# A two-block transformer layer in fp32 on one core: matmuls on high and low parts replaced by plain fp32 matmuls

## The reference

```
# block one
h = rms_norm(x, norm_mix_pre); q, k, v, u, gates = split(h @ w_in)            # 1024 -> 4096
y_a = chunk_band_attention(q, k, v, rel_bias) @ w_attn_out                    # 8 heads of 64
y_b = multiscale_pool(u, w_pool_group, pool_scale) @ w_pool_out
g_a, g_b = split(sigmoid(gates + b_gate))
x = x + rms_norm((g_a * y_a + g_b * y_b) @ w_o, norm_mix_post)
x = x + rms_norm(conv_gated_ffn(rms_norm(x, ..), w_up, conv_w, conv_b, w_down), ..)   # 1024 -> 2*2816 -> 1024
# block two
proj = rms_norm(x, g_mix) @ w_in_2                                            # 1024 -> 3072
h = x + concat(diff_attention(..), neighbourhood_attention(..)) @ w_out
h = h + hier_moe(rms_norm(h, g_ffn), w_rg, w_re, w1, w3, w2)                  # 32 experts, two a token
h = h + rms_norm(p @ w_ple, g_ple) * sigmoid(rms_norm(h, g_plg) @ w_plg)
```

## Time and profile before

| | us |
|---|---|
| median of 3 runs | 1834.44 (1833.17 to 1841.0) |
| the profiled execution | 1832.7 |
| its span, first to last instruction | 1830.9 |
| PE busy | 1599.6 (87%) |
| PE weight loads | 1128.8 (62%) |
| DVE busy | 737.1 (40%) |
| ACT busy | 534.2 (29%) |
| POOL busy | 210.3 (11%) |

### The profile page before, as it was taken

One profiled execution on the slowest core, in us unless ns is written; L12 is line 12 of the kernel. 1 busy time (PEld: TensorE's weight loads), 2 busy tenths in 40 slices (PEclk: granted clock), 3 DMA queues, 4 the chain that ended last, 5 costly groups with the idle time before them and its releaser, 6 DMA issues. The chain is left out here.

```text
span 1830.9 us, 19904 instructions
## 1 busy us (share of the span) xinstructions
PE 1599.6 (87%) x7826; PEld 1128.8 (62%) x7826; DVE 737.1 (40%) x1310; ACT 534.2 (29%) x1012; POOL 210.3 (11%) x204
## 2 busy tenths in 40 slices
PE   5999999879999999787987669698889889888859
PEld 5865688768888888565865558444345345333449
DVE  5225332364444444664439762411113113112363
ACT  4224322344333234332326671211011011010242
POOL 2032010022121111133120100200000000000010
PEclk9988999989999999888999899699999999999979
DMA  7210123113222223021210112468998999999711
GB/s 262 107 36 23 70 94 113 71 63 110 92 92 93 92 92 111 37 95 69 93 38 20 70 37 91 184 253 325 396 358 332 394 347 360 392 368 388 308 38 47
DMA packets 101469, 300.26 MB, mean 164 GB/s; under 512 B 4976, under 2 KB 7152, under 8 KB 90880
## 3 DMA queue, kind: packets, MB, share of 16 engines
q1 hardware_dynamic: 99968, 294.14, 43.1%
q0 software_dynamic: 1408, 4.83, 0.8%
HBM read 296.86 MB, written 2.10 MB: 163 GB/s over the span
## 5 line engine op out<-in xcount | busy, mean ns | idle before, releaser
L514 DVE TENSOR_TENSOR w_lo<-M,w_hi 128x2048 fp32r<-128x2048 f32 x73 | 167.6, 2308 | 215.1 <-ACT w_hi L509 215.1
L2037 PE MATMUL bank<-M 128*64 128x512 f32 x1024 | 229.3, 598 | 26.8 <-DMA M<-in_w 26.3
L699 PE MATMUL bank<-HTH,w_hi 128*128 128x512 f32 x576 | 225.0, 391 | 0.0
L699 PE MATMUL bank<-HTL,w_hi 128*128 128x512 f32 x576 | 224.6, 390 | 0.0
L699 PE MATMUL bank<-HTH,w_lo 128*128 128x512 f32 x576 | 224.5, 390 | 0.0
L509 ACT ACTIVATE w_hi<-M 128x2048 fp32r<-128x2048 f32 x73 | 138.5, 1910 | 192.2 <-PE bank L699 78.4
L2037 PEld LDWEIGHTS bank<-M 128*64 128x64 f32 x1024 | 75.8, 137 | 169.0 <-issue 167.6
L726 PE MATMUL bank<-w_hi,HTH 128*128 128x512 f32 x320 | 129.7, 405 | 20.4 <-DVE M L1400 9.8
L2052 PE MATMUL bank<-M 128*64 128x512 f32 x512 | 116.8, 603 | 25.5 <-DMA M<-in_w 25.0
L726 PE MATMUL bank<-w_lo,HTH 128*128 128x512 f32 x320 | 127.4, 398 | 0.0
L726 PE MATMUL bank<-w_hi,HTL 128*128 128x512 f32 x320 | 127.3, 398 | 0.0
(11 more groups left out here) (270 smaller groups left out, 2746.7 us busy)
## 6 DMA issues: line engine op xcount, KB each, us to landing
M<-in_w SPq DMA_DIRECT2D x192, 1024.0 KB, 11.7
M<-in_wd SPq DMA_DIRECT2D x78, 1024.0 KB, 4.8
M<-in_nb SPq DMA_DIRECT2D x4, 1536.0 KB, 6.3
X<-in_x SPq DMA_DIRECT2D x4, 512.0 KB, 7.6
M<-in_tb POOLq DMA_DIRECT2D x8, 256.0 KB, 4.4
out<-M SPq DMA_DIRECT2D x16, 128.0 KB, 1.9
rowb<-in_rows POOLq DMA_DIRECT2D x3, 512.0 KB, 3.9
M<-in_pT POOLq DMA_DIRECT2D x1, 512.0 KB, 5.2
```

What stands on the lines that cost most here:

```text
L514: e.tensor_tensor(lo[:, :], slots[slot_of[n]], hi[:, :], ALU.subtract).then_inc(split_lo_done, 1)
L699: m = e.matmul(out[:, :], w[:, k0 + k, n0:n0 + 128], v[k], start=(k == 0 and i == 0), stop=(k == len(hi) - 1 and i == 2))
L2037: m = e.matmul(b[64 * s:64 * s + 64, :], Xe[:, 4 * kh + k, o + C * s:o + C * s + C], unit_w(key, 4)[:, k, :], start=(kh == 0 and k == 0), ...
```

## The change

Every product of high and low parts becomes one plain fp32 matmul on the data itself. With it go the copies and subtractions of weights (`split_act`, `split_dve`), those of activations, and the second matmul of gather and scatter. The room they took holds longer rings: `NS` goes from 4 to 6, `NS_MOE` from 7 to 10, `NS_ONCE` from 5 to 2. A dense slot is now free when its matmuls have read it (`unit_read`) instead of when its low part is written. In the feed-forward part POOL writes its product straight into `A`. In the experts the second half of an output is read out of PSUM by DVE and the first by ACT; before, ACT read both for the high part and DVE both for the low part. Norms have one buffer a tile and end at the gain.

```
-NS = 4
+NS = 6
-NS_MOE = 7
-NS_ONCE = 5
+NS_MOE = 10
+NS_ONCE = 2
...
-        def gemm3_T(e, key, n0, out, fills, hi, lo, k0=0):
-            wh, wl = parts(key, KD)
-            for k in range(len(hi)):
-                for i, (w, v) in enumerate(((wh, hi), (wh, lo), (wl, hi))):
-                    m = e.matmul(out[:, :], w[:, k0 + k, n0:n0 + 128], v[k], start=(k == 0 and i == 0),
-                                 stop=(k == len(hi) - 1 and i == 2))
+        def gemm_T(e, w, n0, out, fills, src, k0=0):
+            for k, v in enumerate(src):
+                m = e.matmul(out[:, :], w[:, k0 + k, n0:n0 + 128], v, start=(k == 0), stop=(k == len(src) - 1))
             m.then_inc(fills, 1)
...
             for k in range(4):
-                for i, (src, w) in enumerate(((HTH, wh), (HTH, wl), (HTL, wh))):
-                    m = e.matmul(out[:, :], src[:, 4 * j + k, t * 128:(t + 1) * 128], w[:, k, :],
-                                 start=(j == k == i == 0), stop=(j == 1 and k == 3 and i == 2))
+                m = e.matmul(out[:, :], src[:, 4 * j + k, t * 128:(t + 1) * 128], w[:, k, :], start=(j == k == 0),
+                             stop=(j == 1 and k == 3))
...
         def load_dense(e, n):
             if n >= NS:
-                e.wait_ge(split_lo_done, n - NS + 1)
+                unit_read(e, keys[n - NS])
...
-            if s == 7 and R != 3:
-                e.wait_ge(n_hi, 2 * (NORM_N[R] + t + 1))
-                e.tensor_tensor(HTL[ht_place(t, 1)], norm_y(R, t, 1), HTH[ht_place(t, 1)], ALU.subtract).then_inc(n_lo_v, 1)
...
-            for n in range(8):
-                e.wait_ge(mixed, n + 1)
-                filled(e, ("g", 3, 1, 1))
-                e.activation(HTH[:, n, :], MT[:, n, :], ACT.Copy).then_inc(mt_hi, 1)
...
-            for n in range(8):
-                e.wait_ge(mt_hi, n + 1)
-                e.tensor_tensor(HTL[:, n, :], MT[:, n, :], HTH[:, n, :], ALU.subtract).then_inc(mt_lo, 1)
...
                             for t in range(TT):
-                                for q, v in enumerate((XSH, XSL)):
-                                    m = e.matmul(b[:, kk * 256:(kk + 1) * 256], v[:, t, k * 128:(k + 1) * 128], S[:, t, :],
-                                                 start=(t == 0 and q == 0), stop=(t == 3 and q == 1))
+                                m = e.matmul(b[:, kk * 256:(kk + 1) * 256], XS[:, t, k * 128:(k + 1) * 128], S[:, t, :],
+                                             start=(t == 0), stop=(t == 3))
...
                             for p in SCAT[i]:
-                                for q, Y in enumerate((YH, YL)):
-                                    m = e.matmul(b[:, :], ST[p % 6][:, t * 128:(t + 1) * 128], Y[p % 3][:, h * 512:(h + 1) * 512],
-                                                 start=(p == SCAT[i][0] and q == 0), stop=(p == SCAT[i][-1] and q == 1))
+                                m = e.matmul(b[:, :], ST[p % 6][:, t * 128:(t + 1) * 128], Y[p % 3][:, h * 512:(h + 1) * 512],
+                                             start=(p == SCAT[i][0]), stop=(p == SCAT[i][-1]))
```

More of the change, by code:

```diff
@@ L198, in area @@
             return mem(A0 + o, *shape)
+        HT, XS, S = mem(HT0, KD, NTOK), area(0, TT, D), area(8192, TT, 4 * C)
+        ST = [area(10240 + 512 * i, NTOK) for i in range(6)]
+        Y = [area(13312 + 1024 * i, D) for i in range(3)]
+        OS = area(20704, TT, C)
         o_st = [0]
@@ L567, in norm_act @@
                 e.activation(sq, ms, ACT.Sqrt).then_inc(n_sqrt, 1)
-            if s == 4 and R == 3:
-                e.wait_ge(n_scaled, 4 * R + t + 1)
-                filled(e, ("o2", 3, 1))
-                e.activation(XSH[:, t, :], norm_xs(R, t), ACT.Copy).then_inc(n_keep_hi, 1)
-            if s == 6 and R != 3:
-                if R == 1:
-                    filled(e, ("wo", 3, 1))
-                if R == 2:
-                    filled(e, ("dn", 4, 3, 1))
-                for h in range(2):
-                    taken(e, ("n", R, t, h))
-                    e.activation(HTH[ht_place(t, h)], norm_y(R, t, h), ACT.Copy).then_inc(n_hi, 1)
         def norm_dve(e, R, t, s):
@@ L1078, in wo_pe @@
                     m.then_inc(w_used, 1)
+            ws = [unit_in(e, ("wo", 2 + j), 4) for j in range(2)]
             for t in range(TT):
@@ L1745, in out2_pe @@
                     m.then_inc(w_used, 1)
+            ws = [unit_in(e, ("out2", 2 + j), 4) for j in range(2)]
             for t in range(TT):
@@ L2080, in moe_act @@
                         sc_done(e, i - 3)
-                    for h in range(2):
-                        b, _ = filled(e, ("y2", i, h))
-                        e.activation(YH[i % 3][:, h * 512:(h + 1) * 512], b[:, :], ACT.Copy, scale=WC[i]).then_inc(m_yh, 1)
+                    evac_act(e, Y[i % 3][:, 0:512], ("y2", i, 0), WC[i])
                 if what == "ple":
@@ L2400, in round_pe @@
         for k in range(KD):
-            for i, (t, x) in enumerate([(t, x) for t in range(TT) for x in XS]):
-                m = e.matmul(bank[0][:, k * C:(k + 1) * C], x[:, t, k * 128:(k + 1) * 128], S[:, t, :], start=(i == 0),
-                             stop=(i == 7))
+            for t in range(TT):
+                m = e.matmul(bank[0][:, k * C:(k + 1) * C], XS[:, t, k * 128:(k + 1) * 128], S[:, t, :], start=(t == 0),
+                             stop=(t == 3))
         m.then_inc(o_gath, 1)
```

493 lines of the change are left out of this document (135 added, 358 removed).

## The result

The changed kernel took 2054.67 us in the median of 4 runs (2045.89 to 2059.61), and the kernel before, run beside it, 1837.04 us in 4 runs (1833.17 to 1841.0): a ratio of 1.118, 95% interval 1.113 to 1.123, slower. The prediction was 2059 us, 2033 to 2098. The profiled execution took 2054.93 us, with a span of 2053.2 us. Of medians the change is +217.6 us; of the two profiled executions, on which all that follows rests, it is +222.2.

The account below looks back on a forecast made before the run. PE was taken to bound the dense stages, with PE and DMA close together in the experts. Terms 202.8 + 13.4 + 47 - 11 - 6 - 20.4 = +225.8 us on 1832.7 gave 2058.5, predicted as 2059 us, range 2033 to 2098.

Parts of the forecast that it names:

- The dense term: Dense stages: plain fp32 costs more than three float32r matmuls, +202.8 us at 512 columns and +13.4 us at 256.
- The price of 256 columns: Products at L716 and L2268: 0.43 us per plain fp32 matmul, at most 0.47, against 0.360 us a triple; +13.4 us.
- The experts: Experts' stage: gather and scatter give PE 100.4 us more, partly hidden in 51.3 us of weight waits; +47 us.
- the cover: Experts: longer gather and scatter, with ten slots instead of seven, take in most of the 51.3 us of weight waits.
- the waits for weights stay: Rival, experts: 51.3 us of waits set by latency of a slot's turn; experts +100, total 2112 us; chance 0.07.
- the restarts behind waits: Experts: some 5 us of the 524 us are restarts at the slow clock and go with the waits.
- The norms: Norms: scalings without POOL's subtractions beside them -11 us, PE starting at once and shorter DVE queue -6 us.
- The other borders: Waits at stage borders, in `qk`, the attentions and the experts' tail shrink; -20.4 us, bounds 0 and -45.
- The `qk` term: `qk`: waits of 9.8 us for DVE and 4.1 us for POOL fall by about half, -7 us.
- The freed engines matter more: Rival, attentions and norms: small DVE and ACT work sets these stages; 35 to 50 us more go, about 2018 us; chance 0.09.
- Plain fp32 is cheaper: Rival, dense matmuls: plain fp32 at 0.448 us beats three parts at 0.680 us; total 1532 us; chance 0.02.
- weight loads no longer hide: Rival, matmuls: loads of two records a matmul show, adding more than 60 us; total over 2110 us; chance 0.02.

Follow-up runs that it names:

- Experiment 5: The kernel before with a fourth float32r matmul, low part by low part, added to every dense product; 2105.93 us, ratio 1.149.
- experiment 1: The changed kernel with its ring of expert weights back at 7 slots, five used once (`NS_MOE` 7, `NS_ONCE` 5); 2100.07 us, ratio 1.147.
- experiment 2: The kernel before with its scatter alone in plain fp32, one matmul each, and its expert ring still of seven slots; 1888.07 us, ratio 1.031.
- Experiment 7: The changed kernel with gather and scatter in one float32r matmul each, their low parts left out; 1948.77 us, ratio 1.065.
- experiment 10: The kernel before with the low parts of both halves on DVE and none on POOL in four norms; 1826.04 us, ratio 0.997.
- experiment 12: The changed kernel with an unused POOL subtraction per tile in first and last norm, started behind a tile's second half; 2052.71 us in one run.
- six variants: The changed kernel with seven expert slots, four dense slots, unused ACT and DVE work, single float32r gather and scatter, or unused POOL work (two runs); 1948.77 to 2100.07 us.
- Experiment 4: The changed kernel with 33 unused copies on ACT and 33 unused subtractions on DVE in the feed-forward part; 2047.64 us, ratio 1.119.
- experiment 11: The changed kernel with an unused POOL subtraction per tile in first and last norm, started behind a tile's first half; 2047.01 us in one run.
- experiment 6: The kernel before with two float32r matmuls per dense product, the product of the weights' low part left out; 1612.22 us, ratio 0.881.

## Why the prediction was right

*The dense term, +216.2 us, was right in its size and its reason.* The price of plain fp32 came from sixteen matmuls in another part of the kernel; in 1136 dense ones it is 0.430 us a record. The feed-forward part, which has no wait of PE in either kernel, gave +93.9 for +93. The price of 256 columns was taken between bounds as 0.43 us and is 0.44; the last gate gave +8.7 for +9. Experiment 5 confirms the other price, 0.2265 us. The rows that it is compared with began 4.8 us behind the stage's first matmul; the same stretch here, 458 to 908 us, is 450 us, and the prediction had 449. Over all dense stages the rows are 3.5 us below the 204.0 of the prediction. Waits do not explain that (`wo` kept 1.9 us more than forecast); the stages before had some us more than the price of their matmuls where the granted clock was below 1 (`out2`: 46.4 us for 192 float32r matmuls worth 43.5, at 0.94).

*The experts, +47 us and -1 for their tail, came out at +50.8; the cover was there, but on a condition that the prediction gave only as an aid.* It had the longer work of PE as the cover and the ten slots beside it ("the same bytes need 312 GB/s, well under what the queue moved"). Experiments 1 and 2 show that at seven slots the longer work covers nothing: the waits stay at 46 us while the stage needs 289 to 313 GB/s in its mean. Without the three slots the rival "the waits for weights stay" would have come true, with 2100 us measured for its 2112, and its +100 for the experts is +102.0 there (674.87 - 572.83). Experiment 7 shows the other half: ten slots with short work on PE leave 61.4 us of waits. The cover needs both. The mean of bytes over time was the wrong figure to argue with, for the prediction as for its rival: every wait stands at a DMA share of 1.00 or more, so it is the rate that PE waits for in that stretch, and the slots decide how much is there already. Of the sizes, the restarts behind waits came out as put: PE's busy time grew by 97.5 us where gather and scatter at the measured prices are worth 102.9. The difference to +46 is mostly the dearer gather (0.44 instead of 0.43 us a matmul, some 2.5 us) and the 5.7 us of waits that were left, where the prediction had a few.

*The norms, -17 us, came out at -21.0.* The scalings beside POOL were the right cause (experiments 10 and 12), all 20 at 0.75 us as forecast. PE's waits inside norms fell by 18.0 us. The scalings are 11 us shorter in sum; experiment 10, which frees 9 of those 11 and lengthens DVE's queue, took 9.1 us of the waits. The rest was counted and not tested.

*The other borders, -20.4 us, came out at some -19.* Forecast and measured: entering the gates -0.8 and -0.7 (1.6 to 0.9 us), before `wo` -5.2 and -3.3, entering `out2` -3.4 and -3.3 (4.4 to 1.1 us), `qk` -7 and -7.1 (20.6 to 13.5), the tail of the experts -1 and -0.6 (1.8 to 1.2), the attentions -3 and -4.0, of which the first attention's -2.6 are within the spread of its clock. The one miss is `wo`: the wait was to vanish, and 1.9 us are left, for the product with the gates on DVE (L910). The `qk` term was right in part by luck: it was reckoned as half of 13.9 us, but PE waited 20.6 us there, since the 4.0 us for POOL (L1424) and some smaller waits were not counted. Of its two reasons experiment 5 bears out the one, that tiles come later when PE is slower, and leaves next to nothing for the other, the shorter queue.

*The first attention says nothing.* Its code is the same in the profiled executions of the changed kernel and of its six variants, and it takes 74.4 to 86.1 us there. Two of them (the changed kernel, then experiment 1):

```profile
134.30:217.00 82.70, 75.71 (x313) 42.19 (x313) 40.68 (x161) 36.18 (x105) 25.62 (x27) 0.83 0.09 30
```

```profile
133.40:207.90 74.50, 68.03 (x313) 37.87 (x312) 38.82 (x161) 35.83 (x105) 25.82 (x27) 0.93 0.09 33
```

The granted clock is 0.83 in the one and 0.93 in the other, means of its two levels (1.2 and 2.4 GHz), for the same 313 records of a PE that is idle a tenth of the time. That is most of the spread of the runs, 2046 to 2060 us, and the -3.3 us of the stage table lie inside it.

*The rivals.* "The freed engines matter more" (2018 us) looked for 35 to 50 us in the attentions and the norms. Their rows gave 5 us more than forecast together (-8.0 against -7.2 and -21.0 against -17). Experiment 4 adds that freed work was worth nothing in the feed-forward part, where the rival had not looked. "Plain fp32 is cheaper" and "weight loads no longer hide" are both settled by the 0.430 us between records.

One slip of the working, too small to matter: the sum of 2058.5 us is for the profiled execution, and with the 1.7 us of the median beside it the forecast would have been 2060 and not 2059.

## What to carry to other kernels

Price a change of number format by the distance between starts of a matmul of the same shape somewhere in the same trace, and multiply: where PE is busy without a gap, this held within 1% over 1136 matmuls. Do not judge a wait for a transfer by the stage's mean DMA share: at means of 0.77 and 0.90 every wait stood at a share of 1.00 or more, behind spells in which the queue stood still for want of a free slot. There more slots helped, because the mean left room; at a mean of 0.99 ten slots left 61.4 us of waits. Longer work on the slower side hides a transfer only if there are slots to run ahead into. Work beside a full engine is free only for as long as that engine stays full, so after each cut in the bound engine's work the hidden chains have to be read again.

## What the runs showed of the hardware

POOL and DVE beside each other behave as a lock with a fixed remainder. A scaling that POOL's work holds up ended 0.54 us behind the end of POOL's work in the kernel before (1766.94 and 1766.40), 0.55 in experiment 11 (1975.95 and 1975.40) and 0.55 in experiment 12 (1979.94 and 1979.39), whether it had begun 1.14, 0.24 or 1.02 us ahead of that end. Twelve scalings of the kernel before lie so, all with 0.54 to 0.56 us. Alone it takes 0.75 us, so about 0.2 us of it do not wait for POOL. The Trainium skill ("SBUF — State Buffer", section "SBUF: two separate sides") has the second of the two block until the first is done; the three rows agree with the blocking, and each ends 0.2 us earlier than a full start behind the lock would. It holds the other way round too: in experiment 4 POOL's product of 128x512 took 3.2 us instead of 1.27 where it started beside an unused subtraction of 128x2048 on DVE.

One plain fp32 matmul of 128 x 128 by 512 columns costs 0.86 us and four float32r ones 0.906 us, three 0.680. A kernel that needs only two of the products pays 0.453, where the splits stay hidden: in experiment 6 the gates were 43.6 us shorter for 192 matmuls less, 0.227 us each.

A wait of PE costs more than its length where the granted clock falls behind it: in experiment 1, 39.9 us of added waits brought 11.3 us of slower matmuls in the same 2464 records, at a mean granted clock of 0.97 instead of 0.98.

The 16 DMA engines moved 373 GB/s over 522 us of experiment 7 at a share of 0.99, and 397 in the 24 us of experiment 1 shown above.
